# A third projection ahead of the first attention's scores, and the order of its slots behind it

## The reference, cut to what matters

```
q, k, v = split(u @ w_in + b_in, 3)          # 1024 columns each
for each of 16 heads (64 wide):              # queries attend to all keys of their own and earlier chunks of 64
    s = (q * 64**-0.5) @ k.T + bias[head]    # bias by clipped relative distance
    p = softmax(s)                           # where a key is allowed
    o[head] = p @ v[head]
y = concat(o) @ w_out
```

## Time and profile before

| what | us |
|---|---|
| median of 3 runs | 1029.55 (1028.13 to 1034.27) |
| the profiled execution's own time | 1029.05 |
| its span | 1027.3 |
| TensorE busy | 998.7 (97%) |
| VectorE busy | 802.8 (78%) |
| ScalarE busy | 510.0 (50%) |
| GpSimd busy | 70.1 (7%) |

### The profile page before, as it was taken

One profiled execution on the slowest core, in us unless ns is written; L12 is line 12 of the kernel. 1 busy time (PEld: TensorE's weight loads), 2 busy tenths in 40 slices (PEclk: granted clock), 3 DMA queues, 4 the chain that ended last, 5 costly groups with the idle time before them and its releaser, 6 DMA issues.

```text
span 1027.3 us, 16786 instructions
## 1 busy us (share of the span) xinstructions
PE 998.7 (97%) x6824; PEld 898.8 (87%) x6824; DVE 802.8 (78%) x1253; ACT 510.0 (50%) x684; POOL 70.1 (7%) x147
## 2 busy tenths in 40 slices
PE   7999999999999999999999999999999999999995
PEld 7887778989988799889899898799989989999995
DVE  4688988999788888868886657768884768777776
ACT  3394445344333776635443443644456465555553
POOL 3100220110000122000000000100000000000000
PEclk9999999999999999999999999999999999999999
DMA  8977865899877477834746554354333636655551
GB/s 345 406 275 273 305 248 209 318 363 357 299 277 287 151 294 271 293 120 165 285 168 228 201 183 167 107 205 162 127 135 112 207 101 208 202 186 185 190 196 65
DMA packets 35180, 227.96 MB, mean 222 GB/s; under 512 B 4224, under 2 KB 4352, under 8 KB 10272
## 3 DMA queue, kind: packets, MB, share of 16 engines
q1 hardware_dynamic: 25232, 167.01, 45.7%
q0 software_dynamic: 9872, 59.89, 16.0%
HBM read 225.82 MB, written 1.06 MB: 221 GB/s over the span
## 4 chain that ended last, share of the span: by engine, by line
PE 84%; DVE 8%; ACT 3%; issue 2%; DMA 1%; POOL 1%; POOLq 0%; DVEq 0%; ACTq 0%
PE ps L450 77%; DVE weight_lo L1531 2%; ACT weight_hi L1102 1%; DMA ada_raw<-ada 1%; DVE ada_raw L1547 1%; DVE dev L1685 1%; PE ps L876 1%; DVE dev L1678 1%; DMA weight_raw<-weights 1%; PE ps L982 1%; PE ps L866 1%; PE ps L865 1%; PE ps L695 1%; DVE stat L1689 0%; PE ps L914 0%
## 5 line engine op out<-in xcount | busy, mean ns | idle before, releaser
L1531 DVE TENSOR_TENSOR weight_lo<-weight_raw,weight_hi 128x2048 fp32r<-128x2048 f32 (+3 forms) x191 | 309.5, 1625 | 57.7 <-ACT weight_hi L1102 57.4
L1102 ACT ACTIVATE weight_hi<-weight_raw 128x2048 fp32r<-128x2048 f32 (+2 forms) x168 | 300.3, 1789 | 83.3 <-PE ps L450 61.1
L450 PE MATMUL ps<-act_hi,weight_hi 128*128 128x256 f32 x1336 | 317.9, 281 | 3.3 <-DVE act_lo L1620 1.9
L450 PE MATMUL ps<-act_lo,weight_hi 128*128 128x256 f32 x1336 | 312.7, 277 | 0.0
L450 PEld LDWEIGHTS ps<-act_hi,weight_hi 128*128 128x128 f32 x1336 | 250.3, 187 | 12.7 <-issue 7.7
L450 PEld LDWEIGHTS ps<-act_lo,weight_hi 128*128 128x128 f32 x1336 | 250.4, 187 | 3.2 <-issue 1.0
L450 PE MATMUL ps<-act_hi,weight_lo 128*128 128x256 f32 x1336 | 174.7, 277 | 0.1
L450 PEld LDWEIGHTS ps<-act_hi,weight_lo 128*128 128x128 f32 x1336 | 161.7, 187 | 0.5 <-DVE weight_lo L1531 0.3
L450 PE MATMUL ps<-weight_hi,mlp_hi 128*128 128x512 f32 x256 | 99.8, 390 | 0.0
L450 PE MATMUL ps<-weight_hi,mlp_lo 128*128 128x512 f32 x256 | 99.8, 390 | 0.0
L1547 DVE SCALAR_TENSOR_TENSOR ada_raw<-ada_raw,c_row 128x1024 f32<-128x1024 f32 x80 | 94.4, 1219 | 0.2 <-DMA ada_raw<-ada 0.2
(11 more groups left out here) (320 smaller groups left out, 1323.1 us busy)
## 6 DMA issues: line engine op xcount, KB each, us to landing
weight_raw<-weights SPq DMA_DIRECT2D x144, 1024.0 KB, 5.2
ada_raw<-ada POOLq DMA_DIRECT2D x48, 1024.0 KB, 6.5
weight_raw<-weights SPq DMA_DIRECT2D x23, 512.0 KB, 3.7
row_g<-ln_rows POOLq DMA_DIRECT2D x4, 512.0 KB, 4.3
row_b<-ln_rows POOLq DMA_DIRECT2D x4, 512.0 KB, 5.0
att_bias<-rel_bias POOLq DMA_DIRECT2D x16, 128.0 KB, 5.0
square<-gates POOLq DMA_DIRECT2D x3, 512.0 KB, 4.5
dev<-x_in SPq DMA_DIRECT2D x1, 1024.0 KB, 5.5
```

Source lines behind the costliest of these rows:

```text
L450: return e.matmul(o, a, b, start=start, stop=False, skip_group_check=True)
L1102: e.activation(weight_hi[h][:, 0:size], weight_raw[r][:, 0:size], ACT.Copy).then_inc(hi_full[h], 1)
L1531: ins = e.tensor_tensor(weight_lo[h][:, a + at:b + at], weight_raw[r][:, c], weight_hi[h][:, c].bitcast(F32), ALU.subtract)
```

## The change

TensorE's list: three projections stand ahead of the slots instead of two, and each later one moves a slot forward (`qk(s+3)` in slot s, for slots 0 to 4). The two value halves move from slots 6 and 7 to slots 5 and 6. The values of pairs 4 and 5, which stood behind the slots, take the free place in slot 7, ahead of the turns of that slot's probabilities.

ScalarE's list: in slots 6 and 7 the evacuation of the value half stands ahead of the exponentials instead of behind the weight split. Its other evacuations, its splits, and the lists of VectorE, GpSimd and SyncE are as they were. No instruction is added or removed.

```diff
             v_half(J_ATT, 0, W["av0"], x_ready(1, 0), (1, 2))
             v_half(J_ATT, 1, W["av1"], x_ready(1, 1))
-            for n in range(2):
+            for n in range(3):
                 project(J_ATT + 2 + n, W[f"qk{n}"])
             for slot in range(ATT_PAIRS):
                 heads = (2 * slot, 2 * slot + 1)
                 for h in heads:
                     scores1(h)
-                if slot < 6:
-                    project(J_ATT + 4 + slot, W[f"qk{slot + 2}"])
+                if slot < 5:
+                    project(J_ATT + 5 + slot, W[f"qk{slot + 3}"])
+                elif slot < 7:
+                    v_half(J_ATT + 10, slot - 5, W[f"av{slot - 3}"])
                 else:
-                    v_half(J_ATT + 10, slot - 6, W[f"av{slot - 4}"])
+                    values1(4)
+                    values1(5)
                 if 0 <= slot - 2 < 4:
                     turn_out(slot - 2)
                 if 0 <= slot - 1 < 4:
...
-            values1(4)
-            values1(5)
             e.wait_ge(*emptied(W["y0"]))
             e.wait_ge(*emptied(W["y1"]))
             out1_half(0, 0)
...
             for slot in range(ATT_PAIRS):
                 heads = (2 * slot, 2 * slot + 1)
+                if slot >= 6:
+                    v_out(J_ATT + 10, W[f"av{slot - 4}"], at_v[:, slot - 6, HALF:D], slot - 6)
                 for h in heads:
                     att_exp1(h)
                 if 0 <= slot - 3 < 4:
...
                 split_hi(J_ATT + 6 + slot)
                 if slot < 6:
                     qk(slot + 2)
-                else:
-                    v_out(J_ATT + 10, W[f"av{slot - 4}"], at_v[:, slot - 6, HALF:D], slot - 6)
                 for h in heads:
                     att_turned(h, h, at_pt)
```

## The result

The changed kernel takes 1035.89 us in the median (1033.22 to 1038.31, 20 runs), the kernel before 1030.51 (1028.02 to 1034.27, 20 runs) beside it: a ratio of 1.0048, 95% interval 1.0039 to 1.0056, or about 5 us slower. The forecast was 5.3 us slower, 1034.3; the difference of the medians is 5.4, and the forecast's 1034.3 lies 1.6 under the measured median mostly because it started from 1029.05, the time of one execution, where the kernel before has a median of 1030.51 over 20. Single executions of one kernel differ by as much, so in what follows I measure from a mark to a mark inside one execution.

A forecast was written before the change was run, and what follows sets the result against it. TensorE, busy 97% of the span, was taken as the bound, so only its idle stretches matter. The terms +4.32 + 3.56 + 0 - 2.6 gave +5.3 on 1029.05, so 1034.3 us, range 1030.2 to 1038.8.

The forecast's parts named there:

- Part 1: Before the first scores: the third projection adds 5.47 us but hides the evacuation they waited for, so +4.32.
- part 5: Slot 7 and the output: of 5.62 us of removed work 2.6 come back, the rest lost to late helpers.
- Part 2: Slots 0 to 4: each still holds one projection, its weights and bank ready with 2.8 us or more to spare; cost 0.
- Part 3: Slot 5: the value half waits 2.33 us for its second chunk's high split and 1.37 for its low split; +3.56.
- Part 4: Slot 6: the second value half has both chunks and takes 5.62 us as before; cost 0.
- second way of adding up, by idle time: Whole stretch: idle time removed at the front and added in slot 5, slot 7 and the output, said to give +5.3 too.
- The clock: Slot 5's gaps of 2.3 and 1.4 us leave TensorE at 2.4 GHz; cost 0.
- B: Rival: in slot 5 the helpers split the second value chunk in time, leaving the front's gain, 1027.9 us; chance 0.05.
- E: Rival: projections of slots 0 to 4 lose their cover, +5.3 + 3 to 5, about 1038.5 us; chance 0.08.
- D: Rival: only slot 5 costs, the output's turns meet finished scalings; +3.0, 1032.0 us; chance 0.11.
- C: Rival: the clock falls after slot 5's gaps, +5.3 + 4 to 8, about 1040 us; chance 0.04.

The follow-up runs named there:

- e3: The changed kernel with both e1's earlier weight splits and e2's earlier scalings; ratio to the kernel before 0.9990 (0.9982 to 0.9999).
- e4: The changed kernel with value halves and sums of pairs 4 and 5 put back, three projections still ahead; ratio to the kernel before 1.0050.
- e8: The changed kernel with nine matmuls without a use in slot 5's value half, before the wait for its second chunk; ratio to the kernel before 1.0058.
- e9: As e8, with VectorE's low split also ahead of its modulation chunk in slot 5; ratio to the kernel before 1.0043.
- e1: The changed kernel with ScalarE's and VectorE's weight splits one slot earlier; ratio to the kernel before 1.0006 (0.9996 to 1.0017).
- e2: The changed kernel with VectorE scaling output pairs 4 and 5 ahead of slot 7's modulation chunk and split; ratio to the kernel before 1.0059.
- e7: As e3, with the first output half also ahead of slot 7's turns on TensorE; median 1029.16 us, ratio to the kernel before 0.9995.

## Why the prediction was right

- **Part 1, the front: +4.32 forecast.** The wait of 1.02 went. The front grew by 4.25 to 4.27 in e3, e4, e8 and e9, and by 5.08 or 5.09 in the profiles of the changed kernel, e1, e2 and e7. The 0.8 between the two groups is the pace of the first projections: three in 371.18 - 354.13 = 17.05 in the changed kernel, in 368.63 - 352.20 = 16.43 in e3, where nothing on TensorE's list differs up to there; slot 0's projection makes the other 0.2. The order of the lists isn't the reason, since e8, whose lists are those of the changed kernel up to slot 5 on every engine, took 369.89 - 353.45 = 16.44. What sets that pace wasn't found. It is more than the 0.4 by which the trace's 5.69 passes the forecast; part 5 takes 0.3 back.
- **Part 2, slots 0 to 4: 0 forecast.** No wait of TensorE in them, and slots 2 to 4 are 8.88 long as before; slot 0 is 0.2 longer, by the pace just told.
- **Part 3, slot 5: +3.56 forecast, +3.54 measured**, by 2.15 us of wait and 1.6 of half rate in place of 2.33 and 1.37 of wait. The number came out because both ways end at VectorE's low split, and by some luck: the half ended 0.23 later than forecast, at +9.55, and what stands behind it in the slot took 11.38 - 9.55 = 1.83, where before it took 7.84 - 5.76 = 2.08. e1 shows that the chunk is the cause, e8 and e9 that the low split sets the end.
- **Part 4, slot 6: 0 forecast**, 7.22 against 7.23.
- **Part 5, the output: -2.6 forecast, -2.92 measured.** The waits are 0.26, 0.50 and 1.48 against my 0.4, 0.5 and 1.6, and that for the second scaling 0.4 and not 0.7, since VectorE no longer paused before it. From there on 20.07 in both. (The prediction's second way of adding up, by idle time, gives 5.5 with its own terms and not 5.3; the forecast doesn't hang on it.)
- **The clock: the step failed.** I took 0 from the end of the run, where TensorE was idle for over 4 us at a granted clock of 1.00, and gave the fall a chance of 0.04 with a price of 4 to 8 us. It fell after 2.15 us. That its price was only 0.1 is due to the low split, which was late anyway; I had the mechanism wrong and the price by luck. The Trainium skill, "TensorE: Matmul & The Clock Gate", section "What's actually happening", has half rate as the default state, which activity releases, and gave the right direction here: the trace agrees, the clock fell in the idle stretch and came back once TensorE had worked again for some 3.2 us.
- **The rivals.** B (splits in time) and E (slots 0 to 4 uncovered) didn't occur; D (finished scalings) neither, the wait of 1.48 was there. C occurred in mechanism but not in size.

## What to carry to other kernels

Before moving a stage ahead by one place, write down for each of its inputs when the helper engines make it, measured from the same mark, and what stands ahead of that in their lists: a value half that reads two chunks needs the later one, and that one hadn't moved. Moving the consumer alone cost 5 us; moving the producers with it, splits and scalings, gave that back and at most 0.1% more: 1.2 us of wait saved in front stand against 1.3 us of waits in slot 7. How much of a gain in one slot is lost in a later one has to be looked up each time: in e1 0.74 of 3.94 us came back as wait, in e9 nothing of 0.9.

## What the runs showed of the hardware

- One gap of 2.15 us after steady matmuls took TensorE to 1.2 GHz for some 3.4 us, and a gap of 1.17 us followed by sums of 64 columns did so too (e2), while a gap of 1.48 us in the changed kernel, behind an output product of 512 columns and ahead of four turns and another such product, left it at 2.4 GHz. The length of a gap alone doesn't tell.
- Nor does it tell when the clock falls: with the same gap in slot 5 it fell within the gap in the changed kernel, and some 0.5 us behind its end in e2. In e2's tail it fell 445.2 - 442.65 = 2.5 us behind the gap's end.
- In these runs a fall of the clock cost what wasn't waited for anyway: 0.1 us in slot 5 of the changed kernel and 0.3 in e2's, where the next operand was late, and 1.7 in e2's tail, where the eight high matmuls of an output half and its low ones alone took 449.75 - 445.46 = 4.29 instead of 2.84.
- The same three projections ran in 16.43 or in 17.05 us at a granted clock of 1.00, also between kernels that do not differ up to there. A term of this size can't be read from one pair of profiles.
